# The last layer's expert sums moved onto TensorE, with two experts' rows kept on chip

## What is computed

```python
def deepnorm(x, sub, g, b):
    return layer_norm(DEEPNORM_ALPHA * x + sub, g, b)

# grouped_moe, per token: two experts with gates that sum to 1
gate = gate / gate.sum(-1, keepdims=True)
h = jax.nn.silu(xblk @ w_gate[e]) * (xblk @ w_up[e])
yb = h @ w_down[e]
y = zeros.at[tok_buf].add(yb * gate_buf[:, None])
# end of a layer
x = deepnorm(x, ffn, ln_g[layer, 1], ln_b[layer, 1])
```

## Time and profile before

| | us |
|---|---|
| three runs, median (lowest to highest) | 1181.36 (1179.38 to 1182.4) |
| the profiled execution, its own time | 1174.66 |
| its span in the profile | 1173.0 |

### The profile page before, as it was taken

One profiled execution on the slowest core, in us unless ns is written; L12 is line 12 of the kernel. 1 busy time (PEld: TensorE's weight loads), 2 busy tenths in 40 slices (PEclk: granted clock), 3 DMA queues, 4 the chain that ended last, 5 costly groups with the idle time before them and its releaser, 6 DMA issues.

```text
span 1173.0 us, 13864 instructions
## 1 busy us (share of the span) xinstructions
PE 952.7 (81%) x5241; PEld 499.1 (43%) x5241; DVE 454.5 (39%) x925; ACT 169.4 (14%) x376; POOL 220.9 (19%) x314
## 2 busy tenths in 40 slices
PE   6999969983999698999379899878459977999930
PEld 3444324542555354554134454434235534555510
DVE  1799913553111011111586548564511101111126
ACT  0000021311000000001113332432020000000110
POOL 1094000024211111100431002021240212020022
PEclk8999989985999899999589999978679978999975
DMA  8994349964999999999640003201859999999932
GB/s 252 387 409 157 87 152 414 402 226 170 345 389 403 373 390 384 382 408 411 214 180 1 1 1 144 72 1 68 322 201 392 387 372 391 388 383 395 398 127 107
DMA packets 74301, 313.40 MB, mean 267 GB/s; under 512 B 8797, under 2 KB 19209, under 8 KB 57704
## 3 DMA queue, kind: packets, MB, share of 16 engines
q1 hardware_dynamic: 36752, 228.83, 51.1%
q10 hardware_dynamic: 27352, 55.35, 12.6%
q0 software_dynamic: 10112, 28.06, 6.9%
HBM read 252.48 MB, written 55.31 MB: 262 GB/s over the span
## 4 chain that ended last, share of the span: by engine, by line
PE 58%; DMA 18%; DVE 15%; issue 4%; ACT 2%; POOL 2%; SPq 1%; POOLq 0%; ACTq 0%; DVEq 0%
PE ps L605 20%; PE ps L615 10%; DMA wring<-in_moe_w_gate_dram 8%; DVE arena L859 7%; PE ps L711 7%; PE ps L550 5%; PE ps L730 5%; DMA wring<-in_moe_w_up_dram 3%; PE ps L508 3%; DMA arena<-in_moe_w_up_dram 2%; DMA wring<-in_conv_w_dram 1%; PE ps L756 1%; PE ps L768 1%; DMA xs_dram<-x_sb,place_i 1%; PE ps L782 1%
## 5 line engine op out<-in xcount | busy, mean ns | idle before, releaser
L605 PE MATMUL ps<-wring,arena 128*64 128x256 f32 x2016 | 246.6, 403 | 55.3 <-DVE arena L1011 28.2
L605 PEld LDWEIGHTS ps<-wring,arena 128*64 128x64 f32 x2016 | 152.0, 146 | 149.6 <-issue 56.4
L1536 POOL DMA_DIRECT2D arena<-xs_dram x172 | 91.4, 536 | 357.0 <-DVE arena L1011 336.1
L615 PE MATMUL ps<-wring,arena 128*64 128x512 f32 x560 | 126.7, 594 | 6.2 <-DVE arena L1046 5.7
L508 PE MATMUL ps<-arena,wring 128*128 128x512 f32 x256 | 113.0, 604 | 4.2 <-DMA wring<-in_conv_w_dram 4.2
L1032 DVE COPY arena<-ps 128x256 f32<-128x256 f32 x32 | 13.6, 424 | 251.3 <-PE ps L648 251.3
L859 DVE SCALAR_TENSOR_TENSOR arena<-arena,dwT 128x512 f32<-128x512 f32 x116 | 96.1, 901 | 0.0
L711 PE MATMUL ps<-wring,arena 128*128 128x512 f32 x192 | 86.3, 605 | 3.5 <-ACT arena L1384 2.7
L605 PE MATMUL ps<-arena 128*64 128x256 f32 x736 | 83.2, 380 | 0.8 <-DMA arena<-in_moe_w_up_dram 0.7
L508 PEld LDWEIGHTS ps<-arena,wring 128*128 128x128 f32 x256 | 49.5, 194 | 66.3 <-issue 66.3
L1522 POOL TENSOR_TENSOR rstd<-vareps,half 128x1 f32<-128x1 f32 x20 | 25.7, 1287 | 271.6 <-DVE vareps L875 265.9
(11 more groups left out here) (189 smaller groups left out, 884.6 us busy)
## 6 DMA issues: line engine op xcount, KB each, us to landing
wring<-in_moe_w_gate_dram SPq DMA_DIRECT2D x24, 2048.0 KB, 25.1
wring<-in_moe_w_up_dram SPq DMA_DIRECT2D x24, 2048.0 KB, 19.7
wring<-in_moe_w_down_dram SPq DMA_DIRECT2D x24, 2048.0 KB, 20.2
xs_dram<-zero ACTq DMA_DIRECT2D x2, 16384.0 KB, 65.1
arena<-in_moe_w_up_dram SPq DMA_DIRECT2D x8, 2048.0 KB, 27.9
arena<-in_moe_w_down_dram SPq DMA_DIRECT2D x8, 2048.0 KB, 20.3
arena<-in_moe_w_gate_dram SPq DMA_DIRECT2D x8, 2048.0 KB, 25.7
arena<-xs_dram POOLq DMA_DIRECT2D x172, 64.0 KB, 7.1
```

The source lines that it names most:

```text
L605: mm = pe.matmul(ps[h * CAP:(h + 1) * CAP, bank, 0:256], act[:, k, :], w[:, k, h * 256:(h + 1) * 256], start=(k == 0), stop=(k == KD - 1))
L615: mm = pe.matmul(ps[h * CAP:(h + 1) * CAP, bank, :], act[:, j % 2, (j // 2) * CAP:(j // 2 + 1) * CAP], w[:, j, h * 512:(h + 1) * 512], sta ...
L1536: pool.dma_start(where[q * QROWS:(q + 1) * QROWS, :, :], xs_tiles[q, :, bass.ds(n, 1), :, :]).then_inc(signal, 16)
```

## The change

In layer 1 alone:

- Experts 14 and 15 (`KEPT`) are not stored: their rows stay in `ysb[0]` and `ysb[1]`. Their overflow rows, if any, are stored as before. POOL's gathers wait for one store less on each of the two semaphores, that is up to expert 13's.
- The sum of a tile is made in two PSUM banks on TensorE (`sums`, after the last expert): a diagonal matrix of alpha times x (unscaled now), for each kept expert a matrix `picksT` that has a token's gate where the token's row is in the buffer, times the buffer (64 rows of contraction, one product for each half of the features), and two diagonal matrices of gates times the gathered rows. The gate is zero on a gathered row that is a kept one.
- These matrices are built by VectorE in six parts (`pick`), one after each of the steps of experts 2 to 7, in memory whose former contents are no longer used. TensorE transposes the picks ahead of experts 8 and 9 (`turn_picks`), ACT copies the transposes after the stores of experts 7 and 8. POOL writes a ramp of row numbers (`iota`) once, ahead of the last tile's power in the attention part.
- VectorE's `combine_last` takes statistics and the first scaling from PSUM. ACT's scaling of x by alpha and `gated_y` go.

```diff
--- before.py
+++ after.py
@@ -207,6 +207,17 @@
 
 
         cmp7 = view(AT, E, NBLK - 1)
+
+        KEPT = (E - 2, E - 1)
+        spare = lnrow[:, 0, :, :]
+        diag = spare[:, 0, :].rearrange("p (j t n) -> p j t n", j=2, t=T)
+        hits = spare[:, 1, :].rearrange("p (j t n) -> p j t n", j=2, t=T)
+        picks = resrow.rearrange("p (t i d n) -> p t i d n", t=T, i=2, d=2)
+        picksT = bqrow.rearrange("p (i n) -> p i n", i=2)
+        diag_x = kvrow[:, 0:P]
+        rows_kept = kvrow[:, P:2 * P]
+        place_f, hit, gate_far = (kvrow[:, 2 * P + 8 * i:2 * P + 8 * i + 8].rearrange("p (j t) -> p j t", j=2)
+                                  for i in range(3))
 
 
         ps = ctx.enter_context(nc.psum_tensor("ps", [P, 8, 512], F32))
@@ -286,6 +297,12 @@
         s_xal = sem("s_xal")
         s_y0g = sem("s_y0g")
         s_cmb = sem("s_cmb")
+        s_kept = sem("s_kept")
+        s_picks = sem("s_picks")
+        s_picksT = sem("s_picksT")
+        s_picked = sem("s_picked")
+        s_diag = sem("s_diag")
+        s_sum = sem("s_sum")
 
         s_rope = sem("s_rope")
         s_sin = sem("s_sin")
@@ -617,6 +634,40 @@
                                        w[:, j, h * 512:(h + 1) * 512], start=(j == 0), stop=(j == 3))
                 mm.then_inc(signal, 1)
 
+            def turn_picks(i):
+
+                pe.wait_ge(s_picks, 1)
+                if i:
+                    pe.wait_ge(s_picked, i)
+                for t in range(T):
+                    last = pe.transpose(ps[:, 0, t * P:(t + 1) * P], picks[:, t, i, :, :].rearrange("p d n -> p (d n)"),
+                                        ident[:, :])
+                last.then_inc(s_picksT, 1)
+
+            def sums():
+
+                pe.wait_ge(s_diag, 1)
+                pe.wait_ge(s_picked, 2)
+                pe.wait_ge(s_sg, DEPTH * E)
+                done = pe.snap(g, min_val=1, max_val=4096)
+                for t in range(T):
+                    if t == 2:
+                        pe.wait_ge(s_oyc, done)
+                    for h in range(2):
+                        pe.matmul(ps[:, 2 * t + h, :], diag_x, x_sb[:, t, h * 512:(h + 1) * 512], start=True, stop=False)
+                    for i in range(2):
+                        pe.wait_ge(s_yc, DEPTH * E - 1 + i)
+                        for h in range(2):
+                            part = slice(h * CAP, (h + 1) * CAP)
+                            pe.matmul(ps[:, 2 * t + h, :], picksT[part, i, t * P:(t + 1) * P], ysb[i][part, :],
+                                      start=False, stop=False)
+                    pe.wait_ge(s_yg[t], 32 * DEPTH)
+                    for j in range(2):
+                        for h in range(2):
+                            last = pe.matmul(ps[:, 2 * t + h, :], diag[:, j, t, :], yg[1][t][j][:, h * 512:(h + 1) * 512],
+                                             start=False, stop=(j == 1))
+                    last.then_inc(s_sum, 1)
+
             def experts(l):
                 M0 = E * l
 
@@ -678,6 +729,8 @@
 
                 pe.wait_ge(s_extra, l + 1)
                 for e in range(E):
+                    if l == 1 and 8 <= e < 10:
+                        turn_picks(e - 8)
                     stage_g(e, e % 2)
                     if e:
                         stage_h(e - 1, 1 - e % 2)
@@ -801,6 +854,7 @@
             for u in last_units:
                 unit(u)
             experts(1)
+            sums()
 
 
         @block.vector
@@ -1065,7 +1119,49 @@
 
                 for e in range(2, E):
                     step(e, e // 2, e % 2, last=e == E - 1)
+                    if l == 1 and e < 8:
+                        pick(e - 2)
                 copy_h(E - 1, 1, True)
+
+            def pick(part):
+
+                if part == 0:
+                    dve.wait_ge(s_kept, 1)
+                    own(dve.tensor_copy(place_f, place_i[:, :, :]))
+                elif part < 3:
+                    for t in range(2 * part - 2, 2 * part):
+                        for j in range(2):
+                            ins = dve.tensor_scalar(hits[:, j, t, :], rows_kept, place_f[:, j, t:t + 1],
+                                                    gate_w[:, j, t:t + 1], ALU.is_equal, ALU.mult)
+                    own(ins)
+                elif part == 3:
+                    own(dve.tensor_reduce(hit, hits, AX.X, ALU.add))
+                    own(dve.tensor_tensor(gate_far, gate_w[:, :, :], hit, ALU.subtract))
+                elif part == 4:
+                    both = [hits[:, j, :, :].rearrange("p t (i n) -> p (t i) n", i=2).unsqueeze(2).to_broadcast([P, 2 * T, 2, CAP])
+                            for j in range(2)]
+                    dve.tensor_tensor(picks.rearrange("p t i d n -> p (t i) d n"), both[0], both[1], ALU.add
+                                      ).then_inc(s_picks, 1)
+                else:
+                    dve.tensor_scalar(diag_x, ident[:, :], ALPHA, None, ALU.mult)
+                    for t in range(T):
+                        for j in range(2):
+                            ins = dve.tensor_scalar(diag[:, j, t, :], ident[:, :], gate_far[:, j, t:t + 1], None, ALU.mult)
+                    ins.then_inc(s_diag, 1)
+
+            def combine_last(n):
+
+                for t in range(T):
+                    m = n + t
+                    xt = x_sb[:, t, :]
+                    dve.wait_ge(s_sum, t + 1)
+                    moments(lambda h: ps[:, 2 * t + h, :], m, s_mv)
+                    own(dve.scalar_tensor_tensor(out=xt, in0=ps[:, 2 * t:2 * t + 2, :].rearrange("p a b -> p (a b)"),
+                                                 scalar=mv[:, m, 0:1], in1=lnrow[:, 1, 0, :],
+                                                 op0=ALU.subtract, op1=ALU.mult))
+                    dve.wait_ge(s_rs, m + 1)
+                    dve.scalar_tensor_tensor(out=xt, in0=xt, scalar=rstd[:, m:m + 1], in1=lnrow[:, 1, 1, :],
+                                             op0=ALU.mult, op1=ALU.add).then_inc(s_ln, 1)
 
             def combine(l, n):
 
@@ -1197,7 +1293,7 @@
             table(1)
             experts(1)
             dve.wait_ge(s_rows2, 16 * 2)
-            combine(1, n)
+            combine_last(n)
 
 
         @block.scalar
@@ -1318,6 +1414,8 @@
                     if later or l > 0:
                         act.wait_ge(s_y[b], 32 * (eh + 8 * l))
                     act.activation(ysb[b], ps[:, 4, :], ACT.Copy).then_inc(s_yc, 1)
+                    if l == 1 and e in KEPT:
+                        return
                     act.wait_ge(s_yc, e + (M0 + 1))
                     for h in range(2):
                         act.dma_start(xs_dram[bass.ds(e * S, CAP), h * 512:(h + 1) * 512],
@@ -1343,9 +1441,10 @@
                             act.reg_add(nth, nth, 1)
 
 
-                act.wait_ge(s_scat, 16 * 2 * T * (l + 1))
-                for t in range(T):
-                    act.activation(x_sb[:, t, :], x_sb[:, t, :], ACT.Copy, scale=ALPHA).then_inc(s_xal, 1)
+                if l == 0:
+                    act.wait_ge(s_scat, 16 * 2 * T)
+                    for t in range(T):
+                        act.activation(x_sb[:, t, :], x_sb[:, t, :], ACT.Copy, scale=ALPHA).then_inc(s_xal, 1)
                 act.wait_ge(s_extra, l + 1)
                 silu(0, 0, False)
                 extras(0)
@@ -1355,6 +1454,9 @@
                 for e in range(2, E):
                     silu(e, e % 2, True)
                     store(e - 1, (e - 1) // 2, 1 - e % 2, e > 2)
+                    if l == 1 and 8 <= e < 10:
+                        act.wait_ge(s_picksT, e - 7)
+                        act.activation(picksT[:, e - 8, :], ps[:, 0, :], ACT.Copy).then_inc(s_picked, 1)
                     if l == 0 and 4 <= e < 9:
                         attention_row(e - 4)
                     extras(e)
@@ -1436,8 +1538,6 @@
             norm_rows(1, 1, s_rows2)
             experts(1)
             for t in range(T):
-                gated_y(1, t)
-            for t in range(T):
                 act.wait_ge(s_ln, 3 * T + t + 1)
                 act.dma_start(out_rows[:, t, :], x_sb[:, t, :]).then_inc(s_out, 16)
             act.wait_ge(s_out, 16 * T)
@@ -1568,7 +1668,7 @@
             def combine(l, n):
                 stored = in_register(pool, r_pool, pool.snap(g, min_val=1, max_val=4096) * 32)
                 for b in range(2):
-                    pool.wait_ge(s_y[b], 32 * 8 * (l + 1))
+                    pool.wait_ge(s_y[b], 32 * (8 * (l + 1) - l))
                 pool.wait_ge(s_oy, stored)
 
                 for t in range(T):
@@ -1602,6 +1702,10 @@
             for t in range(T):
                 if t + 1 < T:
                     residual(t + 1)
+                else:
+                    pool.wait_ge(s_kr, T)
+                    pool.iota(rows_kept.rearrange("p (i n) -> p i n", i=2), pattern=[[S, 2], [1, CAP]], base=KEPT[0] * S,
+                              channel_multiplier=0, **exact).then_inc(s_kept, 1)
```

## The result

The changed kernel takes 1172.3 us, the median of 20 runs (1168.41 to 1180.54), against 1180.78 us for the kernel before (20 runs, 1174.77 to 1188.06). The ratio is 0.9932, with a 95% interval of 0.9913 to 0.9951: by that ratio 8.0 us less, between 5.8 and 10.3. The forecast was 1164, that is 17.3 us less, in a range of 1158.5 to 1171.5. The direction was right, the time lies above the range, and the forecast gain is more than twice the measured one.

A forecast was written before the change was run, and what follows sets the result against it. VectorE was taken to bound the tail, before and after: 1128.5 + 4 x 4.70 + 0.3 = 1147.6 against 1164.91, 17.3 us earlier. Taken off the timed median of 1181.36 this gave 1164 us, range 1158.5 to 1171.5.

The forecast's parts named there:

- the price of a product: TensorE's sums in the tail: 0.436 us per product of 512 columns, 3.67 us a tile, bounds 3.5 and 4.4.
- Tile 0's earlier start: Start of the tail: tile 0's sum ready at 1128.5, 10 us ahead of the 1138.54 of before.
- The rule that I set aside: TensorE's sums: the skill's four passes per FP32 product, 0.853 us, would make a tile's sum 8.5 us; chance 0.01.
- Rival (a): Tail: TensorE becomes the bound; at half rate 7.3 us a tile, gain 6.2 (chance 0.03), or near no gain (0.03).
- Rival (e): Tail: gathers do not move ahead, tile 0's rows arrive at 1136 as now; gain 8.1 us, chance 0.03.
- Rival (b): Tail: products show weight load at half clock, 10.9 us a tile; end 8.4 us later than now, chance 0.02.
- The gathers left the path: Before the tail: first gather starts at 1114 to 1117, after expert 13's stores; tile 0's rows covered by at least 2.7 us.
- Tile 3's gather: End of the tail: ready with 1.8 us of slack; as a rival, landing late leaves a gain of 12.1 us, chance 0.08.
- The copy of expert 15: Start of the sums: ScalarE's copy, ready at 1125.22, is needed only 1.4 us in, so it costs nothing.
- my lower bound: Kept-row products on TensorE: two row halves side by side at 0.436 us a pair, 0.87 us a tile.
- The expert loop: Before the tail: picks and transposes cost 0.2 us, bounds 0 and 0.9; rival of larger loss, gain 10.6 at worst, chance 0.08.
- The 4.70 us a tile: VectorE's part in the tail: statistics, mean and variance, power on GpSimd and second scaling; nothing added for reading PSUM.

The follow-up runs named there:

- no_x: Changed kernel without the two products with x of each tile (output incomplete); run once, last expert's end to VectorE's last scaling 26.5 us.
- no_far: Changed kernel without the four products with gathered rows of each tile, gathers still running (output incomplete); run once, last expert's end to VectorE's last scaling 20.6 us.
- x_dve: Changed kernel with alpha times x added by VectorE in PSUM in place of two TensorE products a tile; ratio 0.9896 to the kernel before, 12.3 us less.
- no_far_sbuf: Changed kernel without gathered-row products, VectorE's first scaling reading x from SBUF instead of PSUM (output wrong); last expert's end to VectorE's last scaling 22.6 us.
- all_stored: Changed kernel without kept rows: all experts stored, gathers wait for the last store, TensorE sums six products a tile; ratio 0.9982 to the kernel before.

## Why the prediction was wrong

**The step that failed: the price of a product.** The prediction read "sixteen of the first shape took 6.98 us, 0.436 each" from the earlier trace rows. That row is one `unit` of the attention part, and the loop behind it runs over `k in range(KD)`, with `KD` = 8: eight products. The trace writes two records for each float32 product of this kind: `x16` for eight, `x4` for the two with x, `x8` for the four gathered ones. The expert loop says the same in the kernel's code: `half_products` has 16 products and its rows say `x32`, `down_products` has 8 and its rows say `x16`. So the counts of 32, 16 and 64 products for the expert loop in the description of the kernel before are counts of records; the program has 16, 8 and 32. The `x8` of the earlier trace rows, from which the kept products were priced, are four products likewise. So the price was 6.98 / 8 = 0.87 us, and the sum of a tile 2 x 0.86 + 1.92 + 4 x 0.91 = 7.27 us where I had 3.67, above even my bound of 4.4. With it the tail is TensorE's: 4 x 7.27 + 4.2 = 33.3 us of distance, against 33.5 in the trace. `no_x` (26.5) and `no_far` (20.6) follow from the same price to a tenth. The shortfall comes from this step: the forecast's distance was 1147.6 - 1124.8 = 22.8 us, the trace has 33.5, 10.7 more, and the timed shortfall is 17.3 - 8.0 = 9.3, with an interval of 7 to 11.5. With it the mechanism fell too: VectorE was to bound the tail and hide TensorE, and it is TensorE that bounds it. Tile 0's earlier start made the direction right, with 6.4 us of the 10 forecast.

**The rule that I set aside.** A program product of 512 columns took 0.86 to 0.91 us at a granted clock of 1.00. The Trainium skill (FP8 and Floating Point Precision, TensorE Precision Notes) gives four passes for a true FP32 product, 0.853 us by an estimate from it at 2.4 GHz. By that rule, the trace agrees. The prediction said that the row was half of the rule and let the row decide; the row was right, and I had divided it by the wrong count. A factor of about two between a row and a rule should have sent me to the loop bounds.

**The rivals.** Rival (a), TensorE as the bound with s = 7.3, is what happened, at a gain of 6.2 that the trace puts at 6.8. Its cause was another: the clock was at its full level throughout the sums (1.00 from 1130 to 1160), and s was 7.3 at that clock. It had a chance of 0.03 because it hung on the clock; as "a product costs double", which the loop bounds and the rule both said, it deserved far more. Its difference of 0.6 is mostly the last tile's VectorE part of 4.2 us instead of 4.7. Rival (e) forecast a gain of 8.1, next to the timed 8.0, and that is chance: its gathers stay late, and here they start 8.5 us ahead of the last expert's end. Rival (b)'s sum gives an end 8.3 us later, not 8.4.

**What held.** The gathers left the path: the first started 5.1 us after expert 13's stores were issued, inside the bounds of 1114 to 1117 when shifted by the 5.8 us by which this execution ran late. Tile 3's gather was not waited for, with sums of 7.27 us here and of 5.55 in `x_dve`; no run shows whether it would be with sums as short as forecast. The copy of expert 15 cost nothing. Of the two kept products for an expert, the two halves of 64 rows run side by side: 1.92 us for four, 0.96 a pair against 0.87 for one full product. That is the shape of my lower bound, at double the price. The 8.1 us behind VectorE became 7.6.

The expert loop held too. The timeline after of TensorE shows the transposed picks and the up products of expert 10:

```profile
979.61 0.66 PE L643 MATMUL ps<-ident,rows 128*128 128x128 f32 x4
986.13 6.45 PE L622 MATMUL ps<-wring,arena 128*64 128x256 f32 x32 [5.86 <-DMA wring<-in_moe_w_gate_dram]
...
999.88 7.08 PE L622 MATMUL ps<-wring,arena 128*64 128x256 f32 x64
...
1012.09 0.66 PE L643 MATMUL ps<-ident,rows 128*128 128x128 f32 x4
...
1027.64 3.67 PE L622 MATMUL ps<-arena 128*64 128x256 f32 x32
```

Transposes are single records, and four cost 0.59 us rather than 0.88. The first four lie inside the wait for gate weights, of which 5.86 us are left and which was 6.21, and the clock did not come back (6.45 for 32). From expert 8's overflow block to expert 10's up products are 27.76 us, and before 1021.86 - 994.08 = 27.78: the second group is swallowed by the wait for up weights, which is gone. I had counted 0.2. Over the whole loop the two executions drift by 0.4 us.

**The part of VectorE.** The 4.70 us a tile were wrong by 0.5, in the favourable direction. I added nothing for reading PSUM and did not see that it takes something away: GpSimd's power beside the scaling falls from 1.54 to 0.57 us (`no_far` against `no_far_sbuf`: 4.15 and 4.66 a tile).

## What to carry to other kernels

Before a duration is divided by a count of the profile, set the count beside the bounds of the loop that issued it: here a float32 product is two records and a transpose is one. When work moves from a slow engine to TensorE, write down each engine's time per tile and shift until they are level. The change put 7.3 us on TensorE against 4.2 on VectorE, and giving one pass of 1.24 us back brought 1.72 us a tile (33.5 to 27.7 us in the tail). Work for the first tile can go to the engine that would otherwise wait for it; that alone brought 3.8 us more.

## What the runs showed of the hardware

VectorE with two inputs in SBUF and GpSimd are in each other's way. In `no_far_sbuf` a power on 128 values took 1.54 us beside such a pass, in `no_far` 0.57 us beside the same pass with one input in PSUM. A gather's issue shows it at times: the second gather of tile 3 took 2.00 us beside VectorE's adding passes, and 1.21 in the changed kernel, where it starts 0.4 us before the end of a second scaling, which still reads two inputs from SBUF. But the gather ahead of it in the kernel before, at 1142.07, took 0.98 us though it lay wholly inside such a scaling:

```profile
1141.98 1.34 DVE L894 SCALAR_TENSOR_TENSOR x_sb<-x_sb,rstd,lnrow 128x1024 f32<-128x1024 f32 x1 [0.53 <-POOL rstd L1522]
```

The Trainium skill (SBUF — State Buffer, Who interferes with whom) says that a VectorE instruction with two SBUF inputs contends with a GpSimd instruction that reads SBUF, and that one with at most one SBUF input, outside the two-port modes, does not. By that rule, the trace agrees for the power; the gather's issue of 0.98 us stays open.

TensorE's clock in this tail depends on what the products wait for. In `all_stored`, after a wait of 9.3 us for the gathered rows, four products took 5.58 us, at a clock of 0.50 in the six us up to 1146 and of 0.73 in the six after; the next four, without a wait, took 3.43. In the changed kernel the gathers start ahead of the last expert's end, there is no such wait, and the clock is 1.00. These 2 us or so are a part of what keeping the rows brings beside the sums on TensorE, and they were not in the forecast.
